# A two-layer diffusion backbone on one Trainium2 core: layer 1's residual stream turned to token rows ahead of its router, and squares moved ahead of row copies around the dense layer

## The reference, cut to what matters

```python
def rmsnorm(x, g):
    y = x * lax.rsqrt(jnp.mean(x * x, axis=-1, keepdims=True) + EPS)
    return y * g

def modulate(x, shift, scale):
    return x * (1 + scale) + shift

for i in range(DEPTH):
    sh1, sc1, gt1, sh2, sc2, gt2 = split(silu(c) @ w_mod[i] + b_mod[i], 6)
    ...                                          # token mixing, gives y_x
    x = x + gt1 * rmsnorm(y_x, g_mix_post[i])
    h = modulate(rmsnorm(x, g_ffn_pre[i]), sh2, sc2)
    x = x + gt2 * rmsnorm(ffn(h), g_ffn_post[i])

def moe_swiglu(h, w_r, w1e, w3e, w2e):
    logits = h @ w_r
    vals, idx = lax.top_k(logits, TOP_K)
    comb = sum(one_hot(idx) * softmax(vals))
    for e in range(N_EXPERTS):
        out = out + comb[:, e] * swiglu(h, w1e[e], w3e[e], w2e[e])
```

## Time and profile before

| | us |
|---|---|
| median of three runs | 1728.6 |
| the three runs | 1723.86, 1728.6, 1729.2 |
| the profiled execution, its own time | 1724.4 |
| its span in the trace | 1722.6 |
| TensorE busy | 1630.1 (95%) |
| VectorE busy | 940.2 (55%) |
| ScalarE busy | 528.6 (31%) |
| HBM read | 473.58 MB, 276 GB/s over the span |

### The profile page before, as it was taken

How to read it: one execution, slowest core, us unless ns; L and a number is a source line. 1 busy time by engine, 2 the same in 40 slices (tenths; PEclk the granted TensorE clock), 3 DMA queues, 4 the chain that set the end, 5 groups by cost and what they waited for, 6 DMA issues and landing times.

```text
span 1722.6 us, 21510 instructions
## 1 busy us (share of the span) xinstructions
PE 1630.1 (95%) x8580; PEld 1119.1 (65%) x8580; DVE 940.2 (55%) x1318; ACT 528.6 (31%) x667; POOL 4.0 (0%) x13
## 2 busy tenths in 40 slices
PE   6999999999999999998999999999999999988886
PEld 4688675888888885797878833788348873422222
DVE  6688765544446775699589810898118971100002
ACT  5421334200000005414577601675017740000001
POOL 0000000000000000000000000000000000000000
PEclk9999999999999999999999999999999999999999
DMA  9420976233321326328689999999999999999996
GB/s 337 164 98 1 343 253 227 70 94 95 95 97 37 134 83 213 106 91 294 270 296 370 400 366 420 419 419 421 385 419 420 420 421 416 421 419 420 420 418 267
DMA packets 132571, 476.26 MB, mean 276 GB/s; under 512 B 10626, under 2 KB 41828, under 8 KB 101732
## 3 DMA queue, kind: packets, MB, share of 16 engines
q1 hardware_dynamic: 130640, 474.25, 70.8%
q10 hardware_dynamic: 1812, 0.41, 0.1%
HBM read 473.58 MB, written 1.05 MB: 276 GB/s over the span
## 4 chain that ended last, share of the span: by engine, by line
PE 75%; SPq 9%; DVE 6%; DMA 3%; ACT 3%; issue 3%; ACTq 0%; DVEq 0%; POOL 0%; POOLq 0%
PE ps L949 10%; PE ps L951 10%; PE ps L950 10%; PE ps L1304 8%; PE ps L1419 7%; SPq L816 7%; PE ps L1411 6%; PE ps L1413 6%; PE ps L1354 3%; SPq L820 3%; PE ps L913 2%; PE ps L872 2%; DMA ring<-in_e_w 2%; DMA work<-in_e_w 2%; PE ps L1280 1%
## 5 line engine op out<-in xcount | busy, mean ns | idle before, releaser
L1304 PE MATMUL ps<-ring,work 128*64 128x512 f32 (+1 forms) x1088 | 218.5, 544 | 19.8 <-DMA ring<-in_e_w 17.0
L949 PE MATMUL ps<-ring_rounded 128*128 128x512 f32 (+1 forms) x536 | 190.5, 355 | 2.9 <-DVE norms L2431 1.6
L1304 PEld LDWEIGHTS ps<-ring,work 128*64 128x64 f32 x1088 | 74.4, 136 | 161.0 <-issue 111.5
L2061 DVE TENSOR_TENSOR ring_rounded<-ring,hT_rounded 128x2048 fp32r<-128x2048 f32 (+1 forms) x80 | 165.4, 2086 | 21.1 <-ACT hT_rounded L1943 20.5
L2650 DVE TENSOR_TENSOR norms<-work,ps 128x512 f32<-128x512 f32 (+1 forms) x20 | 11.5, 617 | 282.8 <-PE ps L1304 282.8
L951 PE MATMUL ps<-ring_rounded 128*128 128x512 f32 (+1 forms) x472 | 163.3, 346 | 0.0
L1943 ACT CAST hT_rounded<-ring 128x2048 fp32r<-128x2048 f32 (+1 forms) x80 | 139.5, 1755 | 35.2 <-PE ps L1413 27.8
L951 PE MATMUL ps<-mixT_rounded,ring_rounded 128*128 128x512 f32 x328 | 127.6, 389 | 0.0
L1354 PE MATMUL ps<-ring,mixT 128*64 128x512 f32 x480 | 110.7, 598 | 11.1 <-DMA ring<-in_e_w 11.1
L949 PE MATMUL ps<-mixT_rounded,work_rounded 128*128 128x512 f32 x304 | 118.3, 389 | 0.0
L950 PE MATMUL ps<-hT_rounded,work_rounded 128*128 128x512 f32 x304 | 118.3, 389 | 0.0
(11 more groups left out here) (318 smaller groups left out, 2797.9 us busy)
## 6 DMA issues: line engine op xcount, KB each, us to landing
ring<-in_e_w SPq DMA_DIRECT2D x204, 1024.0 KB, 17.9
ring<-in_e_w SPq DMA_DIRECT2D x112, 768.0 KB, 13.3
ring<-in_w_mod SPq DMA_DIRECT2D x20, 2048.0 KB, 9.7
ring<-in_w_in SPq DMA_DIRECT2D x11, 2048.0 KB, 8.0
ring<-in_w SPq DMA_DIRECT2D x22, 1024.0 KB, 7.9
mixT<-in_e_w SPq DMA_DIRECT2D x18, 1024.0 KB, 20.4
work<-in_e_w SPq DMA_DIRECT2D x18, 1024.0 KB, 20.8
ring<-in_w_mod SPq DMA_DIRECT2D x8, 1024.0 KB, 11.7
```

The lines of the kernel that those rows point to most:

```text
L949: pe.matmul(acc, w_high_, x_high_, start=first, stop=False)
L1304: ins = pe.matmul(narrow_bank(w, b)[H * side:H * side + H, 0:n], xsel[:, k, 0:H], words[:, o:o + n], start=(k == 0), stop=(k == KD - 1), s ...
L2061: return dve.tensor_tensor(dst, src, high, ALU.subtract)
```

## The change

Arithmetic before the experts is regrouped, and work is put in another place of the engines' orders. What it does, from the front:

1. **Start of the dense layer.** Of the chunks (1,1), (1,2), (1,3) one is taken ahead of the squares, the copy of the second stands behind the squares and ahead of 1/rms, the third behind `modulate`; `mod_cols(1, 3)` stands behind the first twenty-four row products.
2. **End of the dense layer.** VectorE adds seven of eight squares instead of four, TensorE takes the sum and the last; tiles 4 and 5 are gated ahead of 1/rms; chunks (1,4), (1,5), (1,6) are placed like those above.
3. **Layer 1's output.** `residual_rows` transposes the latent part of `xT` (four tiles `xa`, sixteen transposes) inside the output projection, and ScalarE copies it to `htok`. The router's weights are multiplied by scale and by shift (`wr_scaled`, `wr_shift`). Behind the projection TensorE takes the shift's logits (eight matmuls, eight columns), the sums of squares with tokens on partitions (four matmuls, one column), sixteen transposes of the branch (`xb`), then 32 matmuls of eight columns for the logits of residual and branch apart, then `mod_rows` of the gate's two chunks and six matmuls of 512 columns for the gate's rows. VectorE joins residual and branch in `htok` and puts the logits together with both 1/rms; `add_branch`, the squares, `normalise` and `modulate` of that norm are gone.
4. **Experts.** The one-hot matrix carries 1/rms of the token; scale and shift are applied behind the gather (four instructions and a copy in place of one or two on each of VectorE and ScalarE, per expert). `arrange` is cut in four and stands inside expert 0. The last step adds `htok` instead of PSUM; its sixteen transposes are gone.
5. **SyncE** waits for `("gate", 0)` ahead of piece 11; pieces 4 to 7 still wait for chunks (1,10) and (1,11), which are now used later.

```diff
@@ TensorE, layer 1's output projection
                 for m in range(3):
-                    accs.append(begin(("y", L, m), m))
+                    accs.append(begin(("y", L, m), m + 3 * L))
                     y_products(accs[m], m, range(0, 4))
+                if L:
+                    for i in range(3):
+                        residual_rows(i)
                 for m in range(3):
                     end(y_products(accs[m], m, range(4, KD)))
+                if L:
+                    residual_rows(3)
...
-                last_square(("yss", 2 * L), n)
-                mods("residual" if L == 0 else "last")
-                square_sum(("ssq", 2 * L + 1), KD, n)
                 if L == 0:
-                    mods("entry")
+                    last_square(("yss", 0), n)
+                    mod_rows(1, 1)
+                    mod_rows(1, 2)
+                    mod_cols(1, 1)
+                    square_sum(("ssq", 1), KD, n)
+                    mod_cols(1, 2)
+                    mod_rows(1, 3)
...
-                    added_squares(("yss", 1), 4, TOK)
-                    mods("second")
+                    last_square(("yss", 1), TOK)
+                    mod_rows(1, 4)
+                    mod_rows(1, 5)
+                    mod_cols(1, 4)
@@ TensorE, behind the projection
+            lg = begin(("lg",), 5)
+            pe.wait_ge(router_scaled, 2)
+            for k in range(KD):
+                pe.matmul(lg[:, 2 * TT * NE:(2 * TT + 1) * NE], ones[:], wr_shift[:, k, :], start=(k == 0),
+                          stop=(k == KD - 1), skip_group_check=True)
...
+            branch_rows(0)
+            branch_rows(1)
+            for side, words in ((0, xT), (1, hT)):
+                for k in range(KD):
+                    for t in range(TT):
+                        o, at_ = CTX + t * P, (side * TT + t) * NE
+                        ins = pe.matmul(lg[:, at_:at_ + NE], words[:, k, o:o + P], wr_scaled[:, k, :], start=False,
+                                        stop=(k == KD - 1), skip_group_check=True)
+            end(ins)
+            for ch in GATES:
+                mod_rows(*ch)
...
+            for i in range(2):
+                acc = begin(("gain", i))
+                end(pe.matmul(acc[:], ones[0:1, :], gate_rows[0:1, 4 * i:4 * i + 4, :], start=True, stop=True))
             for i in range(2):
                 acc = begin(("gate", i))
...
+                pe.matmul(acc[:], ones[0:1, :], gate_words[0:1, 4 * i:4 * i + 4, :], start=True, stop=False)
+                wait_drained(pe, ("mrow", *GATES[i]))
+                end(pe.matmul(acc[:], row_pick, mrow_last if i else mrow, start=False, stop=True))
 
             pe.wait_ge(sel_counted, 1)
@@ ScalarE, end of the dense layer
+                    for m in (4, 5):
+                        gated(("y2", m), m, 0, 5, 0)
                     inverse_rms(("yss", 1), n, D)
-                    for m in range(4, KD):
+                    take_rows((1, 4))
+                    for m in (6, 7):
                         gated(("y2", m), m, 0, 5, 0)
-                    take_rows(*MODS["second"])
@@ ScalarE, layer 1's entry norm
                         square(xT[:, k, :], TOK)
+                    take_rows((1, 5))
                     inverse_rms(("ssq", 2 * L), TOK, D)
-                    take_rows(*MODS["entry1"])
                 modulate(2 * L, L, 0, 0, in_high)
@@ VectorE
-                    split_in(("qk", 1, 0), ("qk", 1, 1), ("qk", 1, 2))
+                    split_in(("qk", 1, 0), ("qk", 1, 1))
+                    for k in range(4, KD - 1):
+                        add_one_square(("yss", 1), k, TOK)
+                    split_in(("qk", 1, 2))
...
             def take_gather(e):
 
                 dve.wait_ge(gather_ready, 2 * e + 1)
-                src = ps[4][:].rearrange("p (m t) -> p m t", m=4)
-                dve.tensor_copy(xsel_high[:, 0:4, :], src).then_inc(xsel_high_ready, 1)
-                dve.tensor_copy(xsel[:, 0:4, :], src)
+                for j in range(4):
+                    ins = dve.tensor_scalar(xsel[:, j, :], ps[4][:, j * P:(j + 1) * P], modv[:, 1, 4, j, 1:2],
+                                            modv[:, 1, 3, j, 1:2], ALU.mult, ALU.add)
+                ins.then_inc(xsel_first, 1)
+                dve.wait_ge(xsel_first, e + 1)
+                dve.tensor_copy(xsel_high[:, 0:4, :], xsel[:, 0:4, :]).then_inc(xsel_high_ready, 1)
                 dve.wait_ge(xsel_high_ready, e + 1)
...
             select(0)
-            arrange()
+            for i in range(2):
+                wait_drained(dve, ("gate", i))
+                dve.tensor_tensor(gate_rows[:, 4 * i:4 * i + 4, :], gate_rows[:, 4 * i:4 * i + 4, :],
+                                  gate_words[:, 4 * i:4 * i + 4, :], ALU.mult)
             take_gather(0)
@@ SyncE
-                        wait_tile(sp, ("mcol", 1, 11) if s == ESLOTS - 3 else ("y", 1, KD - 1))
+                        wait_tile(sp, ("gate", 0) if s == ESLOTS - 3 else ("y", 1, KD - 1))
```

406 lines of the change are left out of this document (264 added, 142 removed).

## The result

The changed kernel took 1740.68 us in the median of five runs (1740.55 to 1745.04), beside 1728.6 for the kernel before (1723.86 to 1729.64): ratio 1.0095, 95% interval 1.0074 to 1.0115. **Slower by 12 us**, above the range of the prediction (1720 to 1734.5). The profiled execution of the changed kernel spans 1738.9 us, that of before 1722.6, so 16.3 us are to be found. In the four larger sets of runs taken later the kernel before had medians of 1725.0 to 1726.7 us, so 12 us is the low end of the loss.

What follows compares the result with a forecast made beforehand. TensorE was taken to bound the kernel up to about 1010 us, then the weight stream, so the end follows expert 0's start. -0.8 - 5.0 + 5.6 - 0.2 = -0.4 us, 1724.4 to 1724.0; named 1728.0, range 1720 to 1734.5.

Steps and rivals of the forecast that it cites:

- Start of the dense layer: Sums of squares begun earlier and `modulate` no longer held by the row copy: -0.8 us (-0.3 to -1.1).
- D: Rival: the end of the dense layer loses its gain, next stage waiting for weights or VectorE; +4, 1732 us; chance 0.06.
- Through the dense layer: Third chunk's transposes behind the row products, 0.45 us, covered by TensorE's earlier 0.96 us wait for VectorE.
- End of the dense layer: Dense layer's closing sums through the entry norm to the next row products: -5.0 us (-3 if sums lag, -5.5).
- Output projection: Sixteen added transposes, twelve ahead of the second halves and four behind: +1.4 us (0.9 to 1.8).
- To the logits: Behind the projection: 18.9 us removed, 104 instructions (15.6 us, about 40 slow) added; logits end 1.8 earlier, projection's 1.4 included.
- Gate's rows: Logits to expert 0: 9.1 us plus some 2.3 ahead of the places, gather -0.7; expert 0 5.6 later, earlier stretch included.
- rival B: The clock stays low from the logits through the gate's rows: total +5 to +6, slower, 1734 us; chance 0.14.
- Experts: VectorE's orders, ScalarE's `take_gather` and SyncE's later pieces cost 0; last four steps out of SBUF some 0.2 us shorter.
- A: Rival: the clock stays up from the projection to the gate's rows; total -8, 1720 us; chance 0.15.
- C: Rival: the ring of expert weights runs dry, the late pieces costing their 9 us; 1737 us; chance 0.03.
- E: Rival: the gate's rows hide because the places wait for VectorE anyway; -5 and more, 1722 us; chance 0.06.

Runs made afterwards that it cites:

- e1: The changed kernel with VectorE's steps for column chunk (1, 2) ahead of the entry norm's scaling and splitting: 1725.89 us, ratio 1.0007 to the kernel before.
- e6: The kernel before with only the end of its dense layer in the changed order: 1718.35 us, ratio 0.9955; in a second set 1719.29, 0.9971.
- e3: e1 with the four gain and gate tiles behind the places of the tokens on TensorE instead of ahead: 1726.58 us, ratio 1.0015.
- e5: e1 with the four one-partition matmuls of the gain and gate tiles reading all 128 partitions: 1722.64 us, ratio 0.9983.
- e2: The changed kernel with the transposes of column chunk (1, 2) written to bank 7 instead of bank 1: 1725.39 us, ratio 1.0004.
- e7: e3 with gain vector and gate bias brought to all partitions by two transfers, VectorE adding and multiplying: 1720.06 us, ratio 0.9960.
- e8: e7 with the first of the two row chunks between the halves of the logits instead of behind them: 1718.96 us, ratio 0.9963.
- e4: e1 without the gate's rows at all (loads, row chunks, tiles, copies, products), output no longer the reference's: 1717.11 us, ratio 0.9958.
- b_shift: The kernel before with eight more small transposes on TensorE at its very start: 1725.15 us, ratio 1.0009.
- b_shift32: The kernel before with 32 more small transposes on TensorE at its very start: 1724.26 us, ratio 0.9988.

## Why the prediction was wrong, point by point

- **Start of the dense layer: the step that failed.** On record -0.8 us, with no wait behind the row chunks but one that was to cover the third chunk's transposes; measured +15.3, a wait of 16.63 us for the bank, and +1.5 more at the low clock. The step counted what each engine had to do and named the third chunk's transposes as the new thing in TensorE's queue. It did not follow the second chunk: its columns were written ahead of the row products, and the step that reads them had been moved behind `normalise` in VectorE's queue. The order of the two engines showed both; the plan of the banks, a list of numbers in the code, showed that `("mcol", 1, 2)` and `("ffg", 0)` share bank 1. None of the rivals had TensorE wait for a bank; D had a stage wait for VectorE, at the other end of the layer and for 4 us. With the bank free (e1) the first row product comes 0.2 us earlier, not 0.8: the sums still end behind VectorE's last tile, and the row copy was not what held ScalarE.
- **Through the dense layer**: the third chunk's four transposes were covered, as forecast. The 0.96 us wait of the earlier trace rows is gone in e1, and the last product starts 0.5 us earlier behind the first than before (360.0 us against 360.5). The table's +0.8 in e1 is the later start of the sum behind it, which e6 shows without those transposes (+1.2). So the start of the layer gives 0.7 us in all once the bank is free, near the 0.8 on record.
- **End of the dense layer**: -5.0, measured -4.5 from the last product against the first profile of before and -3.0 against the second; by the table's row, which begins with the later sum, -5.7 and -4.2. Right in mechanism, and in size against the profile it was worked out from. What it lacked is the wait of 1.06 us for the seventh square: sum and last square hold TensorE for 1.4 us less, not 1.8. The sums (8.60 us for sixteen) keep up with VectorE.
- **Output projection**: +1.4, measured +1.7, and +1.2 against e6.
- **To the logits**: -3.2 without the projection (-1.8 less 1.4; the working on record, 104 x 0.11 + 40 x 0.1, gives 15.4 and not 15.6), measured -4.3 in the changed kernel, -4.4 to -4.6 in e1, e3 and e5, -2.4 in e2 and +0.2 in e7's execution. The clock fell in it, as said, over the last 6.4 us of the logits. The size hangs on where the fall meets them.
- **Gate's rows**: 11.5 us from the logits to the places, measured 11.9 (twelve instructions at 0.48 are 5.8, not the 5.5 on record). The 0.48 us that was taken for one partition was right (0.49). Behind them 0.7 us were to come back; instead 1.8 more went, since the clock fell again in the tiles. This is a half of **rival B**: one-partition matmuls did not hold the clock (e5), and the gather was slow again. But they did not keep it low either: it was at its full value from 869.1 to 875.9, so B's sign, 0.50 through line 1303, did not come, and the work took 11.9 us and not 15. Full height was worth 2.3 us in the stages and 4 in the medians, with intervals that just touch.
- **Experts**: on record -0.2 with the tail, measured -3.6, which goes with the standstill that the kernel before has and the changed one happens not to have. In the profile of before it is one row of 4.6 us, which the prediction did not read. The 0.2 us that the last four steps were to gain out of SBUF are not there: 2.73 us against 2.71.
- **Rivals**: A fell (0.50 from 858.9). C fell: in its first 20 us expert 0 had a transfer share of 1.00 (396 GB/s), and TensorE waited for no piece up to 1000 us, though the pieces 5 to 14 landed 25.5 us later than before and expert 0 began only 19.9 later. D fell in the changed kernel itself and in e6. E fell: TensorE never waited for VectorE's choice. "The end moves by as much as expert 0's start" held: over e1 to e5 and e7 the experts took 850.3 to 851.3 us, whatever the start.
- **By chance right**: with the bank freed the change is at 1.0007, the forecast 1728.0 to 1728.6 is 0.9997. But it is not the forecast sum that came: e1's stages differ from those of before by +1.1, -0.2, +0.8, -5.7, +1.7, -4.5, +10.2 and -3.3, in the order of the table with the last three ahead of the experts added up; so it takes the standstill to make that zero; beside a kernel before that had none, the change would be some 3 us slower.

## What to carry to other kernels

When a step that empties a PSUM bank is moved in one engine's queue, look up who writes this bank next, and put the two side by side: the wait belongs to the pair, and neither engine's own list shows it. Moving work in TensorE's queue is worth only the wait that it covers (2 us at most here); taking it off TensorE, by two transfers made 170 us earlier, was worth 7.5 in the medians and 2.7 in the one profile of each. Before a gain is put down to a change, read the rows whose wait is "issue": here the kernel before lost 4 us to a standstill that edits elsewhere removed, and e8 has it again.

## What the hardware showed that was not expected

- A matmul that reads one partition took as long as one that reads 128 (0.49 against 0.48 us at 512 columns of float32), but the clock fell under a run of four of them in four profiles, and not under four full ones in the one profile of that kind.
- The clock fell to 1.2 GHz while TensorE was at work (busy for 10.20 of 10.20 us at 0.50 in the changed kernel, for 20.40 of 20.40 in e7). In all fourteen profiles it fell in matmuls of one or 8 columns behind 128x128 weights, or within 1.2 us behind them. Where it fell moved from execution to execution (838.3 in e7, 842.7 in e1, 844.8 in e8) and set the length of the 64 instructions of the logits between 9.6 us (e4) and 13.6 (e7).
- TensorE stood for 4.6 to 5.2 us near 1075 us, behind a branch, in three programs out of twelve (the kernel before, b_shift, e8), in all four of their profiles, and at that place in none of the others'. Shorter ones (1.4 to 4.2 us) lie elsewhere in e6, b_shift32, b_shift and the kernel before. Each has a 16 KB packet of an instruction queue begun 2.4 to 2.7 us before its end.
- Up to the first sum of the dense layer all kernels but b_shift and b_shift32 run the same code, and took between 277.2 and 280.8 us for it (b_shift32, with 32 transposes more, 281.6); part of what separates single executions is decided there.
